# Residual stream kept feature-major in a two-block transformer kernel; the bias table loaded later

## The chip, the cores and the metric

The kernel runs on one core of one Trainium2 chip. The metric is the device time of one execution in microseconds. The time of a kernel is the median of its runs.

## The reference

Two blocks in fp32 on 256 tokens of 1024 features, cut to their lines:

```python
def first_block(x, c, ...):                       # 2 layers
    c_act = silu(c)
    for i in range(2):
        sh1, sc1, g1, sh2, sc2, g2 = split(c_act @ w_mod[i] + b_mod[i], 6)
        h = rmsnorm(x, norm_mix[i]) * (1 + sc1) + sh1
        y = pool_mixer(h, w_pool, pool_scale) if i == 0 else attention(h, w_qkv, w_o, rel_bias)
        x = x + g1 * y
        h = rmsnorm(x, norm_mlp[i]) * (1 + sc2) + sh2
        x = x + g2 * (relu(h @ w_up[i]) ** 2 @ w_down[i])      # inner width 4096
    return rmsnorm(x, norm_final)

def second_block(x, meta_tokens, ...):            # 16 meta tokens in front: 272 rows
    h = concatenate([meta_tokens, x])
    proj = rmsnorm(h, attn_norm_w) @ w_in         # gated delta rule and forgetting attention
    h = h + concatenate([o_gdn, o_fox]) @ w_out
    h = h + (silu(n @ w_gate) * (n @ w_up)) @ w_down           # n = rmsnorm(h, ffn_norm_w), 2816
    return rmsnorm(h, final_norm_w)[16:]
```

pool_mixer is a causal mean over 2, 4, 8 or 16 tokens per group of 256 features, minus the token, times a 256 x 256 matrix. The attention has 16 heads of 64 with a T5 bias that depends on the distance. rmsnorm(x, g) is x / sqrt(mean(x^2) + eps) * g over the features of a token.

## The kernel before

Some 193 MB of fp32 weights stream from HBM through four raw slots of 2 MB, in the order in which they are needed. SyncE issues the loads, each when its slot's last reader is done (`free_split`). A tile of weights is a step t (`T_POOL`, `T_MLP0 + i`, `T_QKV + i`, `T_WO`, `T_MLP1 + i`, `T_WIN + i`, `T_WOUT`, `T_FFN + i`) and goes through `split` in four quarters, two to a half: ScalarE (ACT) writes the high part `wh` (type fp32r, L568), VectorE (DVE) the rest `wl` (L1072). TensorE waits for a quarter or a half and makes three passes, high by high, low by high and high by low; `split_used` counts the halves it has read, and the next tile's split of that half waits for it. The activations are split in the same way, into `H` and `L`, both feature-major: eight blocks (k) of 128 features by 256 tokens.

In an up step (`feature_rows`, L1686) the weights are stationary and 256 tokens move: 96 matmuls of 256 columns. In a down step (`down`, L1704) the activations `aTh`, `aTl` are stationary and 512 columns of weights move: 48 matmuls, which add up in the four PSUM banks of y, token-major, over all eight downs of an MLP. The steps run up(0), up(1), down(0), up(2), down(1) and so on to up(7), down(6), down(7); MLP1 has up(8) to down(15) and the last FFN eleven pairs of half the down size. `wo_out` multiplies the mixer's output with w_o or w_out.

The residual stream `x` is token-major, two tiles of 128 tokens by 1024. Where it is updated, the work is one chain, a turn. The gate, a value per feature, is spread over the partitions: `gate_diag` makes eight diagonal matrices on DVE, `gate_mm` multiplies them with ones (L1663), `gate_copy` copies them out of PSUM. `residual` multiplies y with it, tile 0 is added by POOL (L464) and tile 1 by DVE. `stats` on ACT squares and sums a tile and takes the root, `normalise_tile` scales it on DVE, `feature_major` transposes it on TensorE in 16 transposes (L1603), `to_hf` brings it out on ACT with scale and shift (L603), and `split_h` makes `H` and `L` on DVE (L1038, L1055). Then the next tile's first matmuls can start (`parts` waits per two k). Turn 0 stands after pooling, turn 1 before QKV, turn 2 after w_o, turn 3 before W_in (two norms, one after the other, because the first block's final rmsnorm is followed by the second block's first), turn 4 after w_out, turn 5 at the end.

The order of the work is written out by hand, engine by engine. Around turn 1 ACT runs `stats(2)`, then quarters 0 and 1 of the first QKV split, `to_hf`, and quarters 2 and 3; DVE runs `residual` and `normalise_tile`, then quarters 0 and 1, `split_h`, 2 and 3. During MLP0 the modulation of layer 1 is computed too: DVE sums tiles of w_mod that lie in raw slots (`mod_halves`, L962 and L975), and TensorE adds up the partial sums in small matmuls (L1792). The start loads ten tiles of w_mod for layer 0 (`load_mod0`, matmuls L1576), the 2 MB bias table `TB` by POOL's queue from scratch (printed as `arena<-bias_rows`), x, and the pooling weights. `TB` is first read in attention. For the meta tokens the normalised rows `tokm` (DVE, semaphore `xnm_done`) are transposed in eight small transposes and put in front of the 256 tokens in `H` and `L` for W_in; before, both stand in turn 3, and ACT's statistics of them ahead of it.

## Time and profile before

| what | value |
|---|---|
| median of three runs | 1150.83 us |
| the runs | 1149.82 to 1153.22 us |
| span of the profiled execution | 1151.1 us |
| TensorE (PE) busy | 1029.5 us, 89% |
| VectorE (DVE) | 647.9 us, 56% |
| ScalarE (ACT) | 461.3 us, 40% |
| GpSimd (POOL) | 114.3 us, 10% |
| read from HBM | 193.76 MB |

The profile comes from one execution, whose own time is its span. Its first part gives the busy time of each engine; matmuls overlap, so a busy TensorE is not TensorE at its peak. The chain of waits goes from the start to the instruction that ended last and names at each step who held it up; `x96` is a count of instructions, and `out<-in` are the tiles written and read. The rows of stretches give start and end in us, the stretch, the busy us of PE, PEld, DVE, ACT and POOL with their counts, PEclk, the DMA engines' busy share and GB/s. "[2.52 <-ACT wh L568]" at the end of a row is the idle time before it and who ended it. PEclk is the granted clock of TensorE as a share of 2.4 GHz, so 0.50 is 1.2 GHz.

### The profile page before, as it was taken

The page shows a single profiled execution, that of the slowest core. Times are in us where ns is not written, and L with a number is a line of the kernel's source. Part 1 is how long each engine was busy: PE and PEld are TensorE (multiplying, and loading weights), DVE is VectorE, ACT ScalarE, POOL GpSimd, SP SyncE. Part 2 cuts the span into 40 slices and gives each one's busy share as a digit, 9 for nine tenths or more (in the row PEclk, how much of TensorE's full clock was granted, in tenths as well). Part 3 has the DMA queues.
Part 4 walks back from the last instruction along what each step waited for, and adds up shares of the span by engine and source line. Part 5 has one row for each costly group of instructions (what it writes and reads, how often), then busy time and mean ns, then how long its engine had stood idle before and what let it go on. Part 6 is the DMA issues. An engine that isn't in the chain of part 4 may idle for free.

```text
span 1151.1 us, 16537 instructions
## 1 busy us (share of the span) xinstructions
PE 1029.5 (89%) x6589; PEld 905.9 (79%) x6589; DVE 647.9 (56%) x1003; ACT 461.3 (40%) x747; POOL 114.3 (10%) x109
## 2 busy tenths in 40 slices
PE   4588999999898888899999879999579689999996
PEld 1258888997896687799889779987568669999995
DVE  1357677777555975554554556623754535554554
ACT  2234434442534222544444364553311434443443
POOL 3011110021000000111111200001443000000000
PEclk9688999999899558899999979987679899999999
DMA  9997667685637661445455524540000123555520
GB/s 339 333 384 269 220 219 272 240 278 218 236 122 241 222 220 73 147 152 213 163 202 206 181 73 147 194 133 1 1 1 1 37 73 110 175 190 182 194 98 37
DMA packets 105186, 195.60 MB, mean 170 GB/s; under 512 B 2283, under 2 KB 46572, under 8 KB 105132
## 3 DMA queue, kind: packets, MB, share of 16 engines
q1 hardware_dynamic: 104380, 192.58, 47.7%
q0 software_dynamic: 752, 2.26, 0.6%
q8 instruction: 38, 0.62, 0.2%
q14 instruction: 16, 0.13, 0.0%
HBM read 193.76 MB, written 1.07 MB: 169 GB/s over the span
## 4 chain that ended last, share of the span: by engine, by line
PE 78%; DVE 12%; DMA 3%; ACT 3%; issue 2%; POOL 1%; SPq 1%; DVEq 0%; POOLq 0%; ACTq 0%
PE ps L1686 27%; PE ps L1704 15%; PE ps L1940 7%; PE ps L2148 5%; PE ps L1632 4%; PE ps L1827 4%; DMA raw<-in_w_mod 3%; DVE wl L1072 3%; DVE accu L975 2%; ACT arena L585 1%; PE ps L2079 1%; PE ps L1576 1%; PE ps L2090 1%; POOL x L453 1%; PE ps L2089 1%
## 5 line engine op out<-in xcount | busy, mean ns | idle before, releaser
L1072 DVE TENSOR_TENSOR wl<-raw,wh 128x1024 fp32r<-128x1024 f32 (+1 forms) x288 | 315.5, 1138 | 268.4 <-ACT wh L568 268.4
L568 ACT ACTIVATE wh<-raw 128x1024 fp32r<-128x1024 f32 (+1 forms) x288 | 268.4, 983 | 355.3 <-PE ps L1686 187.2
L1686 PE MATMUL ps<-H,wh 128*128 128x256 f32 x864 | 245.0, 284 | 5.9 <-DVE L L1055 5.0
L1686 PE MATMUL ps<-H,wl 128*128 128x256 f32 x864 | 245.2, 284 | 0.0
L1686 PE MATMUL ps<-L,wh 128*128 128x256 f32 x864 | 244.9, 283 | 0.0
L1686 PEld LDWEIGHTS ps<-H,wh 128*128 128x128 f32 x864 | 165.7, 192 | 9.4 <-issue 8.4
L1686 PEld LDWEIGHTS ps<-L,wh 128*128 128x128 f32 x864 | 165.9, 192 | 0.0
L1686 PEld LDWEIGHTS ps<-H,wl 128*128 128x128 f32 x864 | 165.1, 191 | 0.9
L1704 PE MATMUL ps<-wh,aTh 128*128 128x512 f32 x256 | 102.5, 400 | 1.6 <-DVE wl L1072 1.6
L1704 PE MATMUL ps<-wh,aTl 128*128 128x512 f32 x256 | 101.8, 398 | 0.0
L1704 PE MATMUL ps<-wl,aTh 128*128 128x512 f32 x256 | 101.7, 397 | 0.0
L464 POOL TENSOR_TENSOR arena<-arena 128x512 f32<-128x512 f32 x32 | 53.8, 1681 | 310.8 <-ACT arena L613 310.8
L1940 PE MATMUL ps<-H,wh 128*128 128x272 f32 x192 | 57.6, 300 | 2.0 <-DVE L L1055 1.7
L1704 PEld LDWEIGHTS ps<-wh,aTh 128*128 128x128 f32 x256 | 48.4, 189 | 12.7 <-issue 1.6
L1704 PEld LDWEIGHTS ps<-wh,aTl 128*128 128x128 f32 x256 | 48.3, 189 | 11.9
L1940 PE MATMUL ps<-H,wl 128*128 128x272 f32 x192 | 57.3, 299 | 0.0
L1704 PEld LDWEIGHTS ps<-wl,aTh 128*128 128x128 f32 x256 | 48.5, 189 | 11.1
L1940 PE MATMUL ps<-L,wh 128*128 128x272 f32 x192 | 57.2, 298 | 0.0
L1603 PE MATMUL ps<-ident,arena 128*128 128x128 f32 x128 | 22.8, 343 | 24.3 <-DVE arena L1038 19.3
L1576 PE MATMUL ps<-raw,arena 128*32 128x512 f32 x160 | 28.6, 857 | 17.6 <-DMA raw<-in_w_mod 17.6
L1603 PEld LDWEIGHTS ps<-ident,arena 128*128 128x128 f32 x128 | 19.1, 178 | 27.9 <-DVE arena L1038 19.7
L1940 PEld LDWEIGHTS ps<-H,wh 128*128 128x128 f32 x192 | 38.0, 198 | 2.5 <-issue 2.5
(378 smaller groups left out, 1737.4 us busy)
## 6 DMA issues: line engine op xcount, KB each, us to landing
raw<-in_w_up SPq DMA_DIRECT2D x16, 2048.0 KB, 8.6
raw<-in_w_down SPq DMA_DIRECT2D x16, 2048.0 KB, 7.6
raw<-in_w_mod SPq DMA_DIRECT2D x12, 2048.0 KB, 14.9
raw<-in_w_in SPq DMA_DIRECT2D x7, 2048.0 KB, 7.8
raw<-in_w_mod SPq DMA_DIRECT2D x12, 1024.0 KB, 7.0
raw<-in_w_qkv SPq DMA_DIRECT2D x6, 2048.0 KB, 11.2
raw<-in_w_mod SPq DMA_DIRECT2D x8, 1536.0 KB, 7.0
raw<-in_w_gate SPq DMA_DIRECT2D x11, 1024.0 KB, 5.4
```

Source lines behind the costliest of these rows:

```text
L464: e.tensor_tensor(act[:, 2 * b:2 * b + 2, :], r, r, ALU.mult).then_inc(S["a_done"], 1)
L568: e.activation(dst, src, ACT.Copy).then_inc(S["split_h"], 1)
L975: ins = e.scalar_tensor_tensor(out=accu[:, u, :], in0=w[:, k, :], scalar=ccol[:, 0, k:k + 1], in1=accu[:, u, :], op0=ALU.mult, op1=ALU.add)
L1072: e.tensor_tensor(o, src, i1.bitcast(F32), ALU.subtract).then_inc(S["split_l"], 1)
L1576: ins = e.matmul(ps[g:g + 32, b, :], cpad[:, k, :], w[:, k, :], start=(k < 4), stop=(k >= 4))
L1603: ins = e.transpose(ps[:, 4 + k // 2, (k % 2) * SEQ + P * m:(k % 2) * SEQ + P * m + P], tok[:, m, P * k:P * k + P], ident[:, :])
L1632: ins = e.matmul(ps[:, bank, :], src[xa][:, 4 * hb + k, META + P * m:META + P * m + P], w[wb][:, k, :], start=(hb == 0 and k == 0 and n == 0),
L1686: ins = e.matmul(ps[:, 4 + b, SEQ * c:SEQ * c + SEQ], w[wb][:, k, P * c:P * c + P], (H, L)[xa][:, k, META:TT], start=(k == 0 and n == 0), ...
L1704: ins = e.matmul(ps[:, 2 * m + c, :], (aTh, aTl)[xa][buf][:, 2 * hb + k, P * m:P * m + P], w[wb][:, k, 512 * c:512 * c + 512], start=False ...
L1827: ins = e.matmul(ps[:, b + hb, SEQ * c:SEQ * c + SEQ], w[wb][:, k, P * c:P * c + P], (H, L)[xa][:, k, META:TT], start=(k == 0 and n == 0), ...
L1940: ins = e.matmul(ps[:, b + 2 * hb + c, 0:TT], w[wb][:, k, P * c:P * c + P], (H, L)[xa][:, k, :], start=(k == 0 and n == 0), stop=(k == KD ...
L2148: ins = e.matmul(ps[:, 2 * m + c, :], (aTh, aTl)[xa][buf][:, hb, P * m:P * m + P], (wh, wl)[wb][:, hb, 512 * c:512 * c + 512], start=False ...
```

## The change

Everything that touches the residual stream becomes feature-major: `xT`, eight blocks of 128 features by 256 tokens.

- Down steps, the FFN's downs, w_o and w_out make the weights stationary and let 256 tokens move, so that y lies feature-major in PSUM, bank b with the features of k = 2b and 2b + 1. 48 matmuls of 512 columns become 96 of 256; w_o and w_out are split in the column order (`cols=True`).
- A gate is then a scalar per partition: `residual(i, b, gate)` is one DVE instruction per k (y times gate plus x) or, without a gate, one per bank. `gate_diag`, `gate_mm`, `gate_copy` and the additions on POOL go.
- Sums of squares: `squares_of` squares a bank on ACT, `sums` adds it up on TensorE, four fp32 matmuls of two columns per bank with `onw` (ones, and the squared weight of norm_final), `root` on ACT, `rstd` on DVE, and `spread` brings the reciprocal root of each token to all partitions, two matmuls.
- `norm_out` on DVE multiplies x, the weight and the spread root per k, `high` on ACT adds the shift and writes `H`, and DVE writes `L` for k one step behind. `first_half` does the next tile's first half k by k.
- A last down is done by banks of y, with `sums` between them; the two norms of turn 3 need one pass over x, since the second sum of squares is taken with the squared weight (`second_norm`, weight product `w12`). `first_output`, which gives x its first final norm, moves from turn 3 into W_in's step 4 and is eight instructions.
- ACT's and DVE's work at turns 1 to 4 stands in a `turn` on each. In turn 1, `mods_layer1(7, 1)` moves from inside down(7) to behind it, and DVE's `mod_cols1(7)` behind the turn. In turn 0 and the turns the modulation and weight quarters are placed around `norm_out` (turn 0: DVE quarters 0 and 1 of up(0), `norm_out`, quarters 2 and 3).
- Meta tokens: DVE's `tokm` moves behind the whole split of down(14), and the transposes between up(15) and down(14); loading the meta tokens and masks moves ahead of MLP1.
- The start transposes x itself too (16 more transposes, four ACT evictions into `xT`). The table `TB` is issued on POOL behind the first `squares` instead of at the start. At the end x is transposed back in 16 transposes, and the output is stored in four parts instead of two.

```diff
...
     e.dma_start(scratch, ftab[:, :]).then_inc(S["f_out"], 16)
-    e.wait_ge(S["f_out"], 16)
-    e.dma_start(TB, bass.AP(tensor=scratch.tensor, offset=0, ap=[[1, P], [NDIST, HEADS], [1, SEQ]])
-                ).then_inc(S["tb_in"], 16)
...
             e.tensor_tensor(act[:, 2 * b:2 * b + 2, :], r, r, ALU.mult).then_inc(S["a_done"], 1)
     squares(0, first=True)
-    with e.Fori(1, 8) as j:
+    e.wait_ge(S["f_out"], 16)
+    e.dma_start(TB, bass.AP(tensor=scratch.tensor, offset=0, ap=[[1, P], [NDIST, HEADS], [1, SEQ]])
+                ).then_inc(S["tb_in"], 16)
+    with e.Fori(1, 16) as j:
         squares(j)
...
+    def squares_of(i, b):
+        e.wait_ge(S["res"], 8 * i + 2 * b + 2)
+        e.activation((sqT, sqF)[i == 5][:, 2 * b:2 * b + 2, :], xT[:, 2 * b:2 * b + 2, :], ACT.Square
+                     ).then_inc(S["sq_done"], 1)
+    def root(i):
+        e.wait_ge(S["ss_mm"], i + 1)
+        src = ps[:, ss_bank(i), 0:4].rearrange("p (m w) -> p w m", w=2)[:, 0, :]
+        e.activation(stat[:, 1, 0:NM], src, ACT.Sqrt, scale=1.0 / D, bias=epsc[:, :]).then_inc(S["rt_done"], 1)
+    def high(i, ks, shift=None):
+        for k in ks:
+            e.wait_ge(S["t_done"], 8 * i + k + 1)
+            if shift is None:
+                ins = e.activation(H[:, k, META:TT], hf[:, k, META:TT], ACT.Copy)
+            else:
+                ins = e.activation(H[:, k, META:TT], hf[:, k, META:TT], ACT.Identity, bias=shift(k))
+            ins.then_inc(S["hs_h"], 1)
...
+    def turn(i, t, slot, land, shift=None):
+        split(t, slot, land, cols=True, qs=(0, 1))
+        for b in range(4):
+            squares_of(i, b)
+        root(i)
+        high(i, range(4), shift)
+        split(t, slot, land, cols=True, qs=(2,))
+        high(i, range(4, KD), shift)
...
+    def residual(i, b, gate=None):
+        e.wait_ge(*y_ready(i, b))
+        if gate is None:
+            xb = xT[:, 2 * b:2 * b + 2, :]
+            e.tensor_tensor(xb, xb, ps[:, y_bank(i) + b, :].rearrange("p (k t) -> p k t", k=2), ALU.add
+                            ).then_inc(S["res"], 2)
+            return
+        for k in (2 * b, 2 * b + 1):
+            e.scalar_tensor_tensor(out=xT[:, k, :], in0=ps[:, y_bank(i) + b, (k % 2) * SEQ:(k % 2 + 1) * SEQ],
+                                   scalar=gate[:, k:k + 1], in1=xT[:, k, :], op0=ALU.mult, op1=ALU.add
+                                   ).then_inc(S["res"], 1)
+    def rstd(i):
+        e.wait_ge(S["rt_done"], i + 1 if i < 4 else i + 2)
+        e.reciprocal(stat[:, 2, 0:NM], stat[:, 1, 0:NM]).then_inc(S["r2_c" if i == 3 else "rs_done"], 1)
+    def norm_out(i, scale, shift=None, between=None):
+        def low(k):
+            e.wait_ge(S["hs_h"], 8 * i + k + 1)
+            if shift is None:
+                ins = e.tensor_tensor(L[:, k, META:TT], hf[:, k, META:TT], H[:, k, META:TT].bitcast(F32), ALU.subtract)
+            else:
+                ins = e.scalar_tensor_tensor(out=L[:, k, META:TT], in0=hf[:, k, META:TT], scalar=shift(k),
+                                             in1=H[:, k, META:TT].bitcast(F32), op0=ALU.add, op1=ALU.subtract)
+            ins.then_inc(S["hs_l"], 1)
+        for k in range(KD):
+            if k == 0:
+                e.wait_ge(S["bc_mm"], i + 1 if i < 4 else i + 2)
+            e.scalar_tensor_tensor(out=hf[:, k, META:TT], in0=xT[:, k, :], scalar=scale[:, k:k + 1],
+                                   in1=ps[:, ss_bank(i), SEQ:2 * SEQ], op0=ALU.mult, op1=ALU.mult
...
-        nr[0] += 1
-        e.wait_ge(S["gate_set"], gs)
-        def gated(m, c):
...
+    def turn(i, t, slot, scale, gate=None, shift=None, second=None):
+        residual(i, 0, gate)
+        split(t, slot, cols=True, qs=(0,))
+        for b in range(1, 4):
+            residual(i, b, gate)
+        split(t, slot, cols=True, qs=(1,))
+        rstd(i)
+        if second is not None:
+            second()
+        norm_out(i, scale, shift)
+        split(t, slot, cols=True, qs=(2, 3))
+    turn(1, T_QKV, landed(N_QKV)[0], mods[:, 2], modc[:, 0, 40:48], lambda k: modc[:, 1, k:k + 1])
...
     split(T_MLP1 + 14, 3)
+    e.wait_ge(S["sqm_done"], 3)
+    e.tensor_scalar(tokm, xm, stat[0:META, 2, NM:NM + 1], None, ALU.mult).then_inc(S["xnm_done"], 1)
     mlp_low(15, 1)
...
+    def first_output():
+        e.wait_ge(S["r1_set"], 1)
+        for k in range(KD):
+            e.scalar_tensor_tensor(out=xT[:, k, :], in0=xT[:, k, :], scalar=pcol[:, 1, 80 + k:81 + k],
+                                   in1=r1s[:, 0:SEQ], op0=ALU.mult, op1=ALU.mult).then_inc(S["xp_done"], 1)
+    turn(3, T_WIN, landed(N_WIN)[0], w12, modc[:, 1, 40:48], second=second_norm)
...
+    def sums(i, b):
+        e.wait_ge(S["sq_done"], 4 * i + b + 1)
+        for k in (2 * b, 2 * b + 1):
+            for m in range(NM):
+                ins = e.matmul(ps[:, ss_bank(i), 2 * m:2 * m + 2], (sqT, sqF)[i == 5][:, k, P * m:P * m + P],
+                               onw[:, k, :], start=(k == 0 and m == 0), stop=(k == KD - 1 and m == 1))
+        if b == 3:
+            ins.then_inc(S["ss_mm"], 1)
...
+    def spread(i, col=2, bank=None):
+        e.wait_ge(S["rs_done"], i + 1)
+        for m in range(NM):
+            c0 = SEQ + P * m if bank is None else P * m
+            ins = e.matmul(ps[:, ss_bank(i) if bank is None else bank, c0:c0 + P],
+                           stat[:, col, m:m + 1].broadcast_to([P, P]), ident[:, :], start=True, stop=True)
+        ins.then_inc(S["bc_mm"], 1)
...
+    def first_half(i, t, dst, c0=META, early=None):
+        w = [q[:, 0, :].rearrange("p (k n) -> p k n", k=KD) for q in (wh, wl)]
+        for k in range(KD):
+            if k % 4 == 0:
+                quarter(t, k // 4)
+            e.wait_ge(S["hs_h"], 8 * i + k + 1)
+            for c in range(2):
+                for wb in range(2):
+                    e.matmul(dst(c), w[wb][:, k, P * c:P * c + P], H[:, k, c0:TT],
+                             start=(k == 0 and wb == 0 and (c == 0 or c0 == 0)), stop=False)
+            e.wait_ge(S["hs_l"], 8 * i + k + 1)
+            for c in range(2):
+                ins = e.matmul(dst(c), w[0][:, k, P * c:P * c + P], L[:, k, c0:TT], start=False,
+                               stop=(k == KD - 1 and (c == 1 or c0 == 0)))
+                if early is not None and k == KD - 1 and c == 0:
+                    ins.then_inc(early, 1)
+        return ins
...
+        def block(hb, k, f, stop):
             w = [q[:, hb, :].rearrange("p (k n) -> p k n", k=2) for q in (wh, wl)]
-            for c in range(2):
-                for n, (xa, wb) in enumerate(PASSES):
-                    ins = e.matmul(ps[:, 2 * m + c, :], (aTh, aTl)[xa][buf][:, 2 * hb + k, P * m:P * m + P],
-                                   w[wb][:, k, 512 * c:512 * c + 512], start=False, stop=(stop and n == 2))
-                if stop and 2 * m + c < 3:
-                    ins.then_inc(S["y_done"], 1)
+            for n, (xa, wb) in enumerate(PASSES):
+                ins = e.matmul(ps[:, f // 2, SEQ * (f % 2):SEQ * (f % 2) + SEQ], w[wb][:, k, P * f:P * f + P],
+                               (aTh, aTl)[xa][buf][:, 2 * hb + k, :], start=False, stop=(stop and n == 2))
...
-                    for k in range(2):
-                        if m == 0:
-                            quarter(t, 2 * hb + k)
-                        ins = block(m, hb, k, hb == 1 and k == 1)
...
+                    block(1, 0, f, False)
+                    ins = block(1, 1, f, f % 2 == 1)
+                    if f % 2 and f < KD - 1:
+                        ins.then_inc(S["y_done"], 1)
+                    if f == KD - 1:
                         ins.then_inc(S["split_used"], 1)
-                if m == 0 and between is not None:
-                    between()
-            return
-        for hb in range(2):
...
-    down(7, 1, T_MLP0 + 15, last=True, between=lambda: mods_layer1(7, 1))
-    e.wait_ge(S["gate_set"], 4)
-    e.wait_ge(S["mod_col"], 18)
-    feature_major(xn_ready())
-    e.wait_ge(S["res_mul"], 8)
-    fresh[0] = 8
+    down(7, 1, T_MLP0 + 15, last=1)
+    mods_layer1(7, 1)
...
     up(15, T_MLP1 + 13)
+    e.wait_ge(S["xnm_done"], 1)
+    for k in range(KD):
+        ins = e.transpose(ps[:, 6, META * k:META * k + META], tokm[:, P * k:P * k + P], ident[0:META, 0:META])
+    ins.then_inc(S["mtr_done"], 1)
     down(14, 0, T_MLP1 + 14)
...
```

## Rows read from the trace of the kernel before

**Rows 1.** Page, part 1: busy us (share of the span) xinstructions, all engines

```profile
PE 1029.5 (89%) x6589; PEld 905.9 (79%) x6589; DVE 647.9 (56%) x1003; ACT 461.3 (40%) x747; POOL 114.3 (10%) x109
```

**Rows 2.** Chain that ended last, in order of time: start us, us, what; MLP1

```profile
501.24 11.20 PE ps L1704 x48
...
512.43 11.33 PE ps L1686 x96
```

**Rows 3.** Stretches: busy us PE PEld DVE ACT POOL, PEclk, DMA, GB/s

```profile
28.00:34.40 6.40, 1.77 (x16) 1.53 (x15) 0.00 (x0) 0.00 (x0) 0.00 (x0) 0.91 1.05 319
...
45.90:51.30 5.40, 3.64 (x16) 0.59 (x16) 4.36 (x3) 3.61 (x8) 0.00 (x0) 0.50 1.06 388
```

**Rows 4.** Chain in order of time, start and first up step

```profile
33.66 17.62 DMA raw<-in_w_mod
...
90.80 24.69 PE ps L1686 x192
```

**Rows 5.** DMA issues of the whole run: queue, KB each, us to landing

```profile
arena<-bias_rows POOLq DMA_DIRECT2D x1, 2048.0 KB, 15.7
```

**Rows 6.** Timeline of DVE behind turn 0: start, us, line, op, tiles, count

```profile
94.28 5.48 DVE L935 SCALAR_TENSOR_TENSOR arena<-raw,ccol,arena 128x512 f32<-128x512 f32 x7
...
99.67 2.35 DVE L1072 TENSOR_TENSOR wl<-raw,wh 128x1024 fp32r<-128x1024 f32 x2
```

**Rows 7.** Timeline of ACT, turn 0

```profile
87.14 3.75 ACT L603 ACTIVATE hf<-ps,modc,mods 128x256 f32<-128x256 f32 x8
```

**Rows 8.** Chain in order of time, MLP0 and QKV

```profile
188.97 0.78 PE ps L1792 x8
...
271.34 1.78 PE ps L1663 x16
...
294.35 48.02 PE ps L1827 x384
```

**Rows 9.** Timeline of DVE, turn 1

```profile
274.75 1.67 DVE L962 SCALAR_TENSOR_TENSOR arena<-raw,ccol,arena 128x256 f32<-128x256 f32 x4
```

**Rows 10.** Timeline of SyncE, turn 1

```profile
276.44 1.01 SPq L272 DMA_DIRECT2D raw<-in_w_qkv  x2
```

**Rows 11.** DMA issues from 276.0 to 276.5: KB each, us to landing

```profile
raw<-in_w_qkv SPq DMA_DIRECT2D x1, 2048.0 KB, 8.1
```

**Rows 12.** Stretches at turn 1, columns as rows 3

```profile
296.00:298.00 2.00, 2.00 (x11) 2.00 (x11) 1.97 (x4) 1.28 (x2) 0.00 (x0) 0.50 1.04 383
```

**Rows 13.** Chain in order of time, attention to MLP1

```profile
431.47 3.67 PE ps L1603 x16
...
442.46 12.94 PE ps L1632 x48
...
476.57 24.66 PE ps L1686 x192
```

**Rows 14.** Timeline of ACT, start of attention

```profile
366.73 1.28 ACT L695 ACT_TABLE_LOAD   x1
...
368.40 0.40 ACT L695 ACTIVATE arena<-arena,stat 128x128 f32<-128x128 f32 x1 [0.38 <-DVE stat L1231]
```

**Rows 15.** Chain in order of time, last downs of MLP1 and W_in

```profile
636.43 16.11 PE ps L1704 x69
...
673.04 14.74 PE ps L1940 x96
```

**Rows 16.** Timeline of ACT, end of MLP1

```profile
636.53 2.01 ACT L568 ACTIVATE wh<-raw 128x1024 fp32r<-128x1024 f32 x2 [2.52 <-PE ps L1686]
```

**Rows 17.** Timeline of DVE, end of MLP1 and turn 3

```profile
637.62 2.36 DVE L1072 TENSOR_TENSOR wl<-raw,wh 128x1024 fp32r<-128x1024 f32 x2 [3.32 <-ACT wh L568]
...
669.50 0.74 DVE L1302 TENSOR_SCALAR arena<-arena,stat 16x1024 f32<-16x1024 f32 x1
```

**Rows 18.** Timeline of DVE, end of the kernel

```profile
1146.78 1.28 DVE L1549 SCALAR_TENSOR_TENSOR arena<-x,stat,gate 128x1024 f32<-128x1024 f32 x1
```

More of the change, by code:

```diff
@@ L80, in build @@
         L = sb("L", [P, KD, TT], F32R)
-        gate = [sb(f"gate{i}", [P, D]) for i in range(2)]
+        mask_buf = sb("mask_buf", [P, D])
+        wrow = sb("wrow", [P, D])
         ident = sb("ident", [P, P])
@@ L723, in _ @@
                          bias=epsc[0:META, :]).then_inc(S["sqm_done"], 1)
-            stats(4)
-            stats(0, [(S["xp_done"], 1), (S["xp_done"], 2)])
+            mlp_steps(15, 1, T_MLP1 + 13, T_MLP1 + 14, landed(N_MLP1 + 14), None)
+            split(T_MLP1 + 15, *landed(N_MLP1 + 15))
             split(T_WIN, *landed(N_WIN), cols=True, qs=(0, 1))
-            to_hf(pcol[:, 1, 16:24])
-            split(T_WIN, *landed(N_WIN), cols=True, qs=(2, 3))
+            for b in range(4):
+                squares_of(3, b)
+            root(3)
+            e.wait_ge(S["r2_c"], 3)
+            e.activation(stat[:, 6, 0:NM], stat[:, 5, 0:NM], ACT.Sqrt, scale=1.0 / D, bias=epsc[:, :]
+                         ).then_inc(S["rt_done"], 1)
+            high(3, range(2))
+            e.wait_ge(S["bc_mm"], 5)
+            e.activation(r1s[:, 0:SEQ], ps[:, 6, 0:SEQ], ACT.Copy).then_inc(S["r1_set"], 1)
+            high(3, range(2, 4))
+            split(T_WIN, *landed(N_WIN), cols=True, qs=(2,))
+            high(3, range(4, KD))
+            split(T_WIN, *landed(N_WIN), cols=True, qs=(3,))
             for i in range(7):
@@ L904, in _ @@
             split(T_FFN + 21, *g_slot(N_FFN + 21), words=HALF)
-            stats(0, [(S["r2_add"], 6), (S["r2_add"], 8)])
+            for b in range(4):
+                squares_of(5, b)
+            root(5)
         @block.vector
@@ L1156, in _ @@
             scale_cols(1, 0, 112, 4)
-            split(T_MLP0, landed(N_MLP0)[0], cols=True)
-            split_h()
+            split(T_MLP0, landed(N_MLP0)[0], cols=True, qs=(0, 1))
+            e.wait_ge(S["mods_set"], 2)
+            norm_out(0, mods[:, 1], lambda k: modc[:, 0, 24 + k:25 + k])
+            split(T_MLP0, landed(N_MLP0)[0], cols=True, qs=(2, 3))
             mod_sum(10)
@@ L1295, in _ @@
[L1295 to L1302 removed]
             e.wait_ge(S["mtr_done"], 1)
[L1304 removed]
+            e.tensor_tensor(hf[:, :, 0:META], ps[:, 6, 0:KD * META].rearrange("p (k t) -> p k t", k=KD),
@@ L1689, in feature_rows, with up, down @@
                     ins.then_inc(S["split_used"], 1)
-            def up(it, t):
+            def up(it, t, turned=None):
                 first = isinstance(it, int) and it == 0
-                feature_rows(t, None if first else (S["r_done"], 2 * it - 1, "each half"))
-            def down(it, buf, t, last=False, between=None):
+                feature_rows(t, None if first else (S["r_done"], 2 * it - 1, "each half"), turned)
+            def down(it, buf, t, last=None):
                 e.wait_ge(S["tl_done"], 2 * it + 2)
-                def block(m, hb, k, stop):
+                def block(hb, k, f, stop):
@@ L1717, in down @@
+                    return ins
+                for hb in range(2):
+                    if hb == 1 and last is not None:
+                        quarter(t, 3)
+                        for f in range(KD):
+                            block(1, 0, f, False)
[3 more added lines that the diff above has]
+                            if f == KD - 1:
                                 ins.then_inc(S["split_used"], 1)
-                        if m == 0 and between is not None:
-                            between()
@@ L2163, in g_down @@
                 for hb in range(2):
                     half(t, hb)
-                    for m in range(NM):
-                        ins = block(m, hb, False)
+                    for f in range(KD):
+                        for n, (xa, wb) in enumerate(PASSES):
+                            ins = e.matmul(ps[:, f // 2, SEQ * (f % 2):SEQ * (f % 2) + SEQ],
+                                           (wh, wl)[wb][:, hb, P * f:P * f + P], (aTh, aTl)[xa][buf][:, hb, :],
+                                           start=False, stop=(last is not None and hb == 1 and f % 2 == 1 and n == 2))
+                        if last is not None and hb == 1 and f % 2 and f < KD - 1:
+                            ins.then_inc(S["y_done"], 1)
```

580 lines of the change are left out of this document (242 added, 338 removed).

## The prediction, made before the changed kernel was run

> **What bounds the kernel now.** I read the page first: TensorE is busy 89% of the span, the next engine 56% [rows 1]. That is an average over stages with different limits, so the chain of waits in order of time came next. In the MLPs it is TensorE alone, without a gap: a down step of 48 matmuls with 512 moving columns takes 11.20 us, an up step of 96 with 256 columns 11.33 [rows 2]. There only the matmuls themselves count. What is left are the start and the six places where the residual is updated and normalised ("turns": 0 after pooling, 1 before QKV, 2 before MLP1, 3 before W_in, 4 before the last FFN, 5 at the end). In the first 51 us the chain is a DMA of w_mod [rows 4], with the DMA engines full [rows 3]; at each turn TensorE stands still behind DVE and ACT and then starts at the lower clock: at 296 us the granted clock is 0.50 (1.2 GHz) although TensorE is busy again [rows 12]. I then took each turn on its engines' timelines, and its working below is a schedule by the queues as the code orders them, with these unit costs: DVE on 256 columns 1.67/4 = 0.42 us [rows 9], ACT on 256 columns with scale and bias 3.75/8 = 0.47 [rows 7], ACT and DVE per quarter of a weight split 2.01/2 and 2.36/2 [rows 16, 17], four one-column fp32 matmuls (one bank of `sums`) 0.78 [rows 8]. ACT on 512 columns in one instruction I take at 0.6, an estimate between 0.47 and the 1.0 of 1024.
>
> **Down and output weights stationary.** A down becomes 96 matmuls of 256 columns, the form of the up step: 11.33 for 11.20, +0.13 each, 16 times = +2.1; the 11 short downs of the FFN are half as large, +0.7. Together **+2.8** on the path, since nothing else is late there. Bounds: 0 (the two forms alike) and twice that.
> TensorE: Matmul & The Clock Gate, in the section Measured speedup vs the span model, of the Trainium skill says that a weight load overlaps a running matmul only where the row group differs. The change doubles the loads of a down, all of them full height. By that rule the up step, which also loads once per 256 columns, could not run at 118 ns a matmul; the trace contradicts it [rows 2], and the rival that follows from it is priced below.
>
> **The bias table loaded later.** Its 2 MB need 15.7 us in the middle of the saturated stretch [rows 3, 5]; the load rate while it runs is 319 GB/s, 388 later [rows 3]. Its bytes at the later rate are 5.4 us; with the lower rate over some 13 us (13 x (388-319)/388 = 2.3) the later w_mod tiles land up to 7.7 us earlier. What is late next: 16 more transposes of x and four ACT evictions lie before w_mod tile 3's matmuls; 16 transposes at the low clock are 3.67 us [rows 13], the evictions 2.4, but the old wait for that tile was long and only about 2 us of this stick out, on DVE's pooling chain, which had some slack. I take **-6.5** up to the pooling matmuls, bounds -3 and -8. The table now follows the first `squares`; after 100 us the engines have room, and it is read only in attention: 0, at worst 2.
>
> **Turn 0.** The gate's 16 diagonal records and copies go, but TensorE still does four sections of modulation, and now 16 `sums` (4 x 0.78 = 3.1) stand between them. My schedule has the last modulation column ready 0.5 us earlier. Then DVE's `norm_out` is 16 operations of 0.42 = 6.7 us where the old `split_h` was 4.3, and behind it in the queue stand two split quarters, the 5.9 us modulation sum and the split of the next up tile, which began at 99.67 [rows 6]. TensorE reaches that tile early and waits; the old one began up(1) near 104.1, the new one near 102.7 on the same base: **-1.4**.
>
> **Turn 1, a new wait.** `gate_mm(4)`, 1.78 us, goes [rows 8]. But ACT's `turn` now begins with the split of the first QKV tile, and ACT is in order: it first waits until that tile has landed. The tile takes the slot whose last reader is the modulation sum ending at 276.4 [rows 9]; SyncE issues it at 276.44 and it takes 8.1 us [rows 10, 11]: landed 284.5. The last down now starts at 271.34 and reaches its first `sums` (hb 0 plus four columns of hb 1, 72 matmuls) at 279.8. That sum needs ACT's squares, which are queued behind the split: 284.5 + 2.0 + 0.6 = 287.1. TensorE stands 7.3 us **inside** the down. Then, at the low clock: sums 1.8, 12 matmuls 2.5, sums 0.9, 12 matmuls 1.4, two banks of sums and the residual and square of the last bank 2.5, modulation row sum 0.8, root, reciprocal and spread 1.2: `norm_out` from 298.0. It takes 16 x 0.42, plus 0.7 for its first and last and ACT's quarter between, 7.4; the second QKV half waits for two more quarters, 2.4: 307.8, and 5.7 of matmuls: 313.5. Before, these 96 matmuls ended at 294.35 + 48.02 less the 288 that follow at 0.118 = 308.4 [rows 8]. So **+5.1**. If the tile landed before ACT asks, the same schedule gives -5.7.
>
> **Turn 2.** 431.47 to 435.14 the attention output is transposed; then came two rounds of gate matmuls with DVE copies between, until 442.46 [rows 13]. They go. With one ACT and one DVE step on 512 columns, w_o starts at 435.4: -7.0. It starts behind running transposes, so at full clock, another -1.5 (its first 48 took 12.94 for 11.2 [rows 13]). Its 192 narrow matmuls are 22.7 us; after bank 2 come 2.8 of bank 3, three banks of sums 2.5, the rest of bank 3 2.8, residual 0.9, square 0.6, last sums 0.9. ScalarE reloads its table for the square root, but that load runs ahead of the wait of its instruction (loaded at 366.73, waited until 368.40) [rows 14], so only 0.4 of its 1.3 shows; root to spread 1.2; `open_y` 1.8 at the low clock: up(8) starts at 466.8 and its first 48 matmuls end at 474.6. Before: 476.57 + 24.66 less 144 x 0.118 = 484.2 [rows 13]. **-9.6**.
>
> **Turn 3, another wait.** Counted from the start of the last down (636.43 + 11.20 = 647.63), the new schedule has its banks of sums done at 15.6, the double norm (root, five small operations, second root, spread) at 18.0, the first half at 26.7 and the second at 33.7; before it was 673.04 + 14.74, so 40.2 [rows 15]. That is -6.5. But `tokm` moved: TensorE waits for it between up(15) and down(14), and on DVE it stands behind **all four** split quarters of down(14), the last two of which can only start when up(15) is done. The last quarter ended at 637.62 + 2.36 = 639.98, 3.55 after up(15)'s end [rows 15 to 17]; `tokm` adds 0.74 [rows 17], the eight small transposes 1.0 to 1.3 (half of rows 13's, an estimate): 5.3 of TensorE at rest or at small work, plus 1.4 for the lower clock after it (at 1.2 GHz the 5 us before 299 cost about half of themselves [rows 12]; part of that time falls on the transposes). -6.5 + 5.3 + 1.4 = **+0.2**.
>
> **Turns 4 and 5.** No gate there before. Fewer evictions (-0.6) against narrow matmuls and 16 sums between: **-0.2** (bounds -2, +2). At the end 3.1 of sums and 16 transposes replace two token-wise sums of squares; the last scaled output, which ended 1.28 after 1146.78 [rows 18], I find at 1148.2: **-0.1** (bounds -2, +2).
>
> Sum: +2.8 - 6.5 - 1.4 + 5.1 - 9.6 + 0.2 - 0.2 - 0.1 = -9.7. From the execution's own 1151.1 that is 1141.4; the median of the runs is 0.3 lower: **1141**. DVE's extra `first_output` in W_in (8 x 0.42 = 3.4) falls where the convolution's 5 us stood one step before; 0, at worst 2.
>
> **Rivals.**
> 1. The two new waits don't bite (the tile is early, or ACT's order is harmless; `tokm` gets through between quarters). For: each rests on a few us of schedule. Against: the landing and the order on DVE stand in the rows [rows 9, 10, 11, 17]. Turn 1 alone: 1141 - 10.8 = 1130; turn 3 alone: 1134; both: 1123. Chance 0.14.
> 2. The start gives nothing: the transposes of x, ACT's evictions and the pooling chain take the DMA's place, or the table collides with the first MLP tiles. 1141 + 6.5 = 1147.5. For: DVE's chain there is long. Against: the w_mod tiles are awaited again and again. Chance 0.15.
> 3. Slower: `norm_out` is a ping-pong, DVE's product, ACT's high part, DVE's low part for each k. I let it overlap (0.84 per k, ACT's 0.47 hidden under the next product). If the hand-overs don't overlap, a k costs 0.42 + 0.47 + 0.42 and two hand-overs, about 1.5: 5 turns x 8 x 0.66 = +26: 1167. It decides from 1.08 per k on (9.7/40 above 0.84). Chance 0.08.
> 4. Exposed weight loads: the 768 + 264 added loads at the about 0.12 us between matmuls of the up step would be +124: 1265. Chance 0.01.
> 5. That the change doesn't do what it says would be a table still loaded in the start; that is case 2.
>
> **How the numbers follow.** Forecast 0.62, its own range 1134 to 1148 from the bounds above; rivals 0.14, 0.15, 0.08, 0.01. The range for 8 in 10 takes in turn 1's rival and case 2: 1130 to 1151. A difference under 0.3% (3.5 us) can't be told from none here: faster is below 1147.4. Of the forecast 0.58 is faster, of case 1 all, of case 2 half: 0.79; the same 0.12; slower 0.09.
>
> **What would show it.** Right: one down form at 118 ns a matmul; w_mod 3 landed before 32 us, up(0) near 82; a gap of 7 us inside the last down of MLP0 that ends with ACT's split and square; no gap between transposes and w_o; 4 us before down(14) released by DVE at the line of `tokm`. Wrong: no gap inside down(7); a k of `norm_out` over 1.0; up(0) at 90 as before.

## The result, and the profile after

The changed kernel took 1170.8 us (median of four runs, 1168.1 to 1174.2) against 1150.8: 1.0169 of the time before, 95% interval 1.0148 to 1.0189. The forecast was 1141, the range 1130 to 1151. Run again beside the last experiments it took 1166.4, 1.0115 (1.0099 to 1.0132). So it is slower by 1 to 2%, and neither the forecast nor the range held. One run of e1 (1479 us) and one of e4 (3343 us) stand in no ratio. The profiled execution has a span of 1166.4, 15.3 above the 1151.1 of before; the ledger below is made of these two.

The page's part 1 of the changed kernel, columns as [rows 1]:

```profile
PE 1059.1 (91%) x7917; PEld 992.8 (85%) x7917; DVE 635.4 (54%) x1002; ACT 460.3 (39%) x733; POOL 101.9 (9%) x101
```

The other engines have less to do than before, TensorE 29.6 more. The added matmuls of the downs are not the reason: in MLP1 five pairs of steps take 113.3 for 112.7. The chain of waits, in order of time (start, duration, what), by turn:

```profile
66.90 4.52 PE ps L1628 x32
71.42 3.61 PE ps L1594 x16
...
99.38 1.42 DVE arena L966
...
116.05 11.30 PE ps L1742 x96
...
288.10 2.00 ACT wh L574 x2
...
290.67 1.87 PE ps L1628 x8
292.54 2.77 PE ps L1742 x12
...
315.58 40.03 PE ps L1859 x336
...
449.47 6.86 PE ps L1688 x48
...
507.13 11.30 PE ps L1742 x96
...
646.67 1.45 DVE arena L1300
648.17 1.03 PE ps L1928 x8
649.20 20.31 PE ps L1742 x156
...
951.21 3.35 PE ps L1628 x24
954.56 5.34 PE ps L1696 x24
```

L1628 is `sums` (a fp32 matmul has two records, so x8 is one bank), L1742 the down step, L1594 the modulation rows, L1859 QKV, L1300 `tokm`, L1696 w_out. Where such landmarks stand in both chains, the span can be cut into stretches:

| stretch | before | after | difference | forecast |
|---|---|---|---|---|
| start to turn 0's gate (DVE's product of gate and scale) | 64.5 | 60.9 | -3.7 | -6.5 |
| to down(0): turn 0, up(0), up(1) | 51.0 | 55.2 | +4.2 | -1.4 |
| down(0) to down(5) | 121.1 | 122.9 | +1.8 | +0.6 |
| down(5) to QKV's fifth tile: turn 1 | 105.8 | 116.7 | +10.9 | +5.5 |
| to the attention output's transposes: code not changed | 89.1 | 90.0 | +0.9 | 0 |
| to down(8): turn 2 | 69.8 | 61.6 | -8.2 | -9.6 |
| down(8) to down(13) | 112.7 | 113.3 | +0.6 | +0.6 |
| down(13) to the end of W_in: turn 3 | 152.0 | 154.7 | +2.7 | +0.6 |
| to w_out: nearly all of it code not changed | 152.3 | 154.6 | +2.3 | 0 |
| w_out to the FFN's first down: turn 4 | 58.9 | 62.1 | +3.2 | -0.2 |
| the rest | 174.1 | 174.6 | +0.5 | +0.6 |

The misses have one thing in common, which the rows of stretches show (start:end, stretch, busy us of PE, PEld, DVE, ACT and POOL with counts, PEclk, DMA share, GB/s). Of the changed kernel:

```profile
66.80:71.40 4.60, 4.60 (x37) 4.58 (x41) 0.00 (x0) 1.07 (x3) 0.00 (x0) 0.77 1.05 386
71.40:83.60 12.20, 10.77 (x50) 4.65 (x49) 0.17 (x1) 3.25 (x5) 0.00 (x0) 0.50 0.87 311
...
290.60:302.00 11.40, 11.20 (x52) 11.11 (x52) 3.48 (x7) 1.91 (x4) 0.00 (x0) 0.50 1.05 387
302.00:311.00 9.00, 7.80 (x36) 7.53 (x36) 4.75 (x13) 3.93 (x8) 0.00 (x0) 0.50 0.09 33
...
951.20:954.60 3.40, 3.40 (x26) 3.32 (x26) 0.79 (x2) 1.23 (x2) 0.00 (x0) 0.82 0.76 239
954.60:959.90 5.30, 5.29 (x24) 4.99 (x24) 0.00 (x0) 0.00 (x0) 0.00 (x0) 0.50 0.00 0
```

In the first row TensorE is busy all the time, with `sums`, and the granted clock falls from 1.0 to 0.50 (1.2 GHz) inside it. In the third and fourth it stays at 0.50 for 20 us though TensorE works. In the last two it falls during w_out's sums, and there TensorE is busy without a gap from 937 on; in turn 0 it had stood still for 0.7 us until 65.9. Summed over stretches of 2 us, (1 - PEclk) x 2 x PE busy gives the microseconds that TensorE worked at the low clock: 176 before, 206 after. At half speed 29.4 more are 14.7 us of time. That this is close to the 15.3 of the spans is in part chance: the second profile of the changed kernel (e10) has 200, 11.9 us of time, where its span is 18.1 longer. The ledger's misses hold waits as well.

Theory: the two-column matmuls of `sums` leave or keep TensorE at the low clock. Rival: the idle time around each turn does, and the sums' shape is of no matter. Beside it stand the two waits of the forecast, in turns 1 and 3, and the table's place.

### The profile page after: what moved, and what is told of

The parts are those of the page before. It is cut to its first block, busy times and chain, and to the rows that moved or that the text cites. A ratio compares the mean times of both kernels' runs of the same rounds, so it can differ in the third digit from the quotient of the medians.

```text
span 1166.4 us, 19172 instructions
## 1 busy us (share of the span) xinstructions
PE 1059.1 (91%) x7917; PEld 992.8 (85%) x7917; DVE 635.4 (54%) x1002; ACT 460.3 (39%) x733; POOL 101.9 (9%) x101
## 4 chain that ended last, share of the span: by engine, by line
PE 78%; DVE 13%; ACT 3%; DMA 3%; issue 2%; SPq 1%; POOL 0%; DVEq 0%; ACTq 0%
PE ps L1725 23%; PE ps L1742 14%; PE ps L1969 6%; PE ps L2175 5%; PE ps L1859 3%; PE ps L1696 3%; DVE wl L1114 3%; DMA raw<-in_w_mod 2%; PE ps L1628 2%; PE ps L1668 2%; DVE accu L1006 2%; PE ps L1651 1%; PE ps L1594 1%; PE ps L1688 1%; PE ps L2108 1%
## 5 line engine op out<-in xcount | busy, mean ns | idle before, releaser
L1114 DVE TENSOR_TENSOR wl<-raw,wh 128x1024 fp32r<-128x1024 f32 (+1 forms) x288 | 316.8, 1141 | 278.7 <-ACT wh L574 278.7
L1725 PE MATMUL ps<-H,wh 128*128 128x256 f32 x816 | 228.6, 280 | 2.5 <-DVE wl L1114 1.6
L1725 PE MATMUL ps<-H,wl 128*128 128x256 f32 x816 | 229.7, 282 | 0.0
L1725 PEld LDWEIGHTS ps<-H,wh 128*128 128x128 f32 x816 | 154.2, 189 | 3.2 <-issue 3.2
L1742 PE MATMUL ps<-aTh,wh 128*128 128x256 f32 x512 | 147.4, 288 | 1.6 <-DVE wl L1114 1.6
L1742 PE MATMUL ps<-aTh,wl 128*128 128x256 f32 x512 | 146.2, 285 | 0.0
L1742 PE MATMUL ps<-aTl,wh 128*128 128x256 f32 x512 | 145.9, 285 | 0.0
L1742 PEld LDWEIGHTS ps<-aTh,wh 128*128 128x128 f32 x512 | 99.5, 194 | 1.6 <-issue 1.6
L1742 PEld LDWEIGHTS ps<-aTl,wh 128*128 128x128 f32 x512 | 99.3, 194 | 0.0
L1742 PEld LDWEIGHTS ps<-aTh,wl 128*128 128x128 f32 x512 | 99.3, 194 | 0.0
L2175 PE MATMUL ps<-aTh,wh 128*128 128x256 f32 x176 | 49.3, 280 | 0.0
L2175 PE MATMUL ps<-aTh,wl 128*128 128x256 f32 x176 | 49.1, 279 | 0.0
L2175 PE MATMUL ps<-aTl,wh 128*128 128x256 f32 x176 | 49.1, 279 | 0.0
L1628 PE MATMUL ps<-onw,arena 128*128 128x2 f32 x192 | 28.2, 274 | 12.8 <-ACT arena L594 12.7
```

Of the source, the lines that this page charges most:

```text
L1114: e.tensor_tensor(o, src, i1.bitcast(F32), ALU.subtract).then_inc(S["split_l"], 1)
L1628: ins = e.matmul(ps[:, ss_bank(i), 2 * m:2 * m + 2], (sqT, sqF)[i == 5][:, k, P * m:P * m + P], onw[:, k, :], start=(k == 0 and m == 0), s ...
L1725: ins = e.matmul(ps[:, 4 + b, SEQ * c:SEQ * c + SEQ], w[wb][:, k, P * c:P * c + P], (H, L)[xa][:, k, META:TT], start=(k == 0 and n == 0), ...
L1742: ins = e.matmul(ps[:, f // 2, SEQ * (f % 2):SEQ * (f % 2) + SEQ], w[wb][:, k, P * f:P * f + P], (aTh, aTl)[xa][buf][:, 2 * hb + k, :], st ...
L2175: ins = e.matmul(ps[:, f // 2, SEQ * (f % 2):SEQ * (f % 2) + SEQ], (wh, wl)[wb][:, hb, P * f:P * f + P], (aTh, aTl)[xa][buf][:, hb, :], st ...
```

## The experiments

**The sums by themselves (e7, e8).** 32 fp32 matmuls that compute nothing, between down(13) and up(15), where TensorE never idles; two moving columns, then 64:

```diff
+            for n in range(32):
+                e.matmul(ps[:, 7, 0:2], ident[:, :], onw[:, 0, :], start=True, stop=True)
             up(15, T_MLP1 + 13)
```

> Changed kernel with 32 extra fp32 matmuls of 2 moving columns, reading constants and written to an unused bank, between down(13) and up(15), in a stretch where TensorE is never idle and the granted clock is 1.0. It measures the sums by themselves. Theory A: the granted clock falls to 0.50 during or right behind them though TensorE is never idle: the matmuls cost 6.2 at full clock, and they and the first microseconds of up(15) take 3 to 6 more: 1180 to 1184. Theory B (only idle time lowers the clock): clock stays 1.0, 6.2 more, 1177.

> As e7, but each of the 32 matmuls moves 64 columns. Theory A: the clock stays at 1.0, and as each matmul is bounded by its issue or load at about 0.2 us, the cost is the 6.2 to 6.9 of the matmuls alone: 1177.5. Theory B: the same as e7. If e7 and e8 both lose the clock, 64 columns are too few as well, and e1's gain has another cause.

Measured: 1185.2 and 1177.3 us (two runs each), 1.0291 and 1.0222 of before. Chain and stretches of e7, then of e8:

```profile
635.99 11.22 PE ps L1926 x64
647.21 13.66 PE ps L1725 x96
...
631.00:636.00 5.00, 5.00 (x46) 5.00 (x44) 2.36 (x2) 1.39 (x2) 0.00 (x0) 1.00 0.88 338
636.00:641.00 5.00, 5.00 (x35) 5.00 (x35) 2.46 (x3) 3.34 (x5) 0.00 (x0) 0.73 0.11 15
641.00:647.20 6.20, 6.20 (x31) 6.20 (x30) 0.00 (x0) 0.00 (x0) 0.00 (x0) 0.50 0.88 329
```

```profile
630.95 7.09 PE ps L1926 x64
638.04 11.43 PE ps L1725 x96
...
631.00:634.50 3.50, 3.50 (x34) 3.50 (x33) 2.43 (x3) 3.32 (x5) 0.00 (x0) 1.00 0.02 5
634.50:638.00 3.50, 3.50 (x33) 3.50 (x33) 0.04 (x1) 0.00 (x0) 0.00 (x0) 1.00 0.69 211
```

With two columns the clock falls to 0.50 while TensorE is 100% busy, and 32 times more moving columns cost less: 7.09 for 11.22, and the up step behind them 11.43 for 13.66. That is theory A, by 6.4 us in the profiles. The Trainium skill (TensorE: Matmul & The Clock Gate, section Why this matters for your kernels) names idle gaps between matmul bursts as what to avoid; here there is none, and the measurement decides: narrow matmuls alone are enough.

**Wide sums in the kernel (e1).**

```diff
-                        ins = e.matmul(ps[:, ss_bank(i), 2 * m:2 * m + 2], (sqT, sqF)[i == 5][:, k, P * m:P * m + P],
-                                       onw[:, k, :], ...
+                        ins = e.matmul(ps[:, ss_bank(i), 64 * m:64 * m + 64], (sqT, sqF)[i == 5][:, k, P * m:P * m + P],
+                                       onw[:, k, :].unsqueeze(2).broadcast_to([P, 2, 32]), ...
```

> Changed kernel (median 1170.8) with one edit: each matmul of `sums` moves 64 columns (each of the two weights 32 times) instead of 2; the number of matmuls stays, and only one copy of each result is read. Theory A: the 16 two-column matmuls of each turn count as almost no work for the clock gate, so the granted clock falls to 0.50 while TensorE is busy (turn 0 from 68 us on, turn 4 at 954) or stays there (turn 1 from 290 to 310). In the changed kernel 19 us of busy time in turn 0, 20 in turn 1 and 18 in turn 4 run at the low clock, before it was 6, 7 and 15; at 64 columns most of it goes and half of each microsecond comes back: about 6 + 5 + 2, so 1158. Theory B: the clock is low because TensorE stood idle before each turn, and how wide the sums are does not matter: 1171, the granted clock as in the changed kernel. If the wider matmuls cost more than the narrow ones, the 24 quarters of sums show it: each of the 96 matmuls of turns 0 to 5 took 0.195 us at full clock.

Measured: 1158.3 us, 1.0045 (1.0023 to 1.0067), 12 below the changed kernel's first median and 8 below its second. By stretches: gate to down(0) 52.8 for 55.2, turn 1 113.9 for 116.7, turn 4 59.3 for 62.1. Its w_out keeps the full clock, sums and matmuls behind them:

```profile
946.40:949.30 2.90, 2.90 (x26) 2.82 (x26) 0.78 (x2) 1.23 (x2) 0.00 (x0) 1.00 0.98 308
949.30:952.20 2.90, 2.86 (x24) 2.66 (x23) 0.00 (x0) 0.00 (x0) 0.00 (x0) 1.00 0.00 1
```

The rival falls for turn 4: its stretch took 62.1 or 62.2 in all eight profiles with narrow sums and 59.3 or 59.4 in all four with wide ones. In turn 0 the wide sums did not hold the clock in this profile:

```profile
69.20 4.87 PE ps L1628 x32
```

They held it in e5 (3.62) and e6 (3.63) and not in e12 (6.04), while it fell inside the narrow ones in all eight profiles. One-column modulation sums stand before and behind them, so that the width alone decides there is not shown. Nor is it in turn 1, where the narrow profiles lie between 114.4 and 116.7.

**Turn 1's wait (e2).**

```diff
 def turn(...):      # ACT, for i == 1
-    split(t, slot, land, cols=True, qs=(0, 1))
     for b in range(4):
         squares_of(i, b)
     root(i)
+    split(t, slot, land, cols=True, qs=(0, 1))
```

and on DVE, for i == 1:

```diff
     residual(i, 0, gate)
-    split(t, slot, cols=True, qs=(0,))
     for b in range(1, 4):
         residual(i, b, gate)
-    split(t, slot, cols=True, qs=(1,))
     rstd(i)
+    split(t, slot, cols=True, qs=(0, 1))
```

> Changed kernel with one edit: in turn 1 ACT does its four squares and the root before quarters 0 and 1 of the first QKV split, and DVE takes its two quarters behind the reciprocal. Theory A: in the changed kernel TensorE stands from 282.4 to 290.7 inside the last down because ACT waits for the QKV tile, which lands at 288.1, and then works at the low clock until 310. Without the wait the sums end near 287, both quarters are split by 291.3 and the second QKV half starts near 301 instead of 315.6: 1157. Rival: the tile lands at 288.1 whatever is done, its splits, norm_out and the clock decide; then the gain is 3 us or less, 1168 or more.

Measured: 1151.1 us, 1.0017 (0.9984 to 1.0049), 20 below the changed kernel's first median and 15 below its second. Chain:

```profile
263.03 18.49 PE ps L1749 x156
281.55 0.89 DVE xT L1074 x2
283.14 1.05 PE ps L1635 x8
284.20 1.52 PE ps L1749 x12
...
303.94 40.03 PE ps L1866 x336
```

The 8.3 us at rest inside the last down are gone, 12 matmuls take 1.52 where they took 2.77, and down(5) to QKV's fifth tile is 104.5 for 116.7 (114.4 to 116.7 in the seven profiles with narrow sums and without the edit). The rival (the tile's landing decides) falls. Another 5.9 of this profile's 16.5 are in the stretch W_in to w_out, 148.7 for 154.6, which the edit doesn't touch.

**`tokm` early (e3).** On DVE:

```diff
             e.reciprocal(stat[0:META, 2, NM:NM + 1], stat[0:META, 1, NM:NM + 1]).then_inc(S["sqm_done"], 1)
-            split(T_MLP1 + 14, 3)
             e.wait_ge(S["sqm_done"], 3)
             e.tensor_scalar(tokm, xm, stat[0:META, 2, NM:NM + 1], None, ALU.mult).then_inc(S["xnm_done"], 1)
+            split(T_MLP1 + 14, 3)
```

> Changed kernel with one edit: DVE's reciprocal and `tokm` (the meta tokens) stand before the four split quarters of down(14) instead of behind them. Theory A: TensorE's 6.1 us between up(15) (ends 643.1) and down(14) (starts 649.2) are DVE's last two quarters and `tokm`; with `tokm` early only the 1.0 of small transposes stays, and the 1.4 to 1.9 lost to the lower clock behind the gap go too: 6 to 7 us less, 1164.5. Rival: down(14) would have waited for its own split anyway, or the time is given back at the last down's banks: under 2 us, 1169 or more.

Measured: 1159.9 us, 1.0074 (1.0046 to 1.0102), 11 below the changed kernel's first median and 6 below its second, whose interval it touches. The stretch of turn 3 is what shows the gain: 145.9, where the six profiles without the edit or added matmuls lie between 154.6 and 154.8. Chain, up(15) and then the downs:

```profile
632.66 11.36 PE ps L1725 x96
644.62 18.58 PE ps L1742 x156
```

0.6 instead of 6.1 lies between them, the transposes in it, and 156 matmuls take 18.58 for 20.31, as the clock no longer falls.

**The table's place (e4, e9).** Undone in the changed kernel, and made alone in the kernel before:

```diff
             squares(0, first=True)
+            e.wait_ge(S["f_out"], 16)
+            e.dma_start(TB, ...).then_inc(S["tb_in"], 16)
```

> Changed kernel with one part undone: the bias table is loaded at the start again, as in the kernel before. Theory A: the later table brings the pooling forward by 3.7 us (its last DVE step at 61.0 instead of 64.7), but in turn 0 the loss at the low clock eats it, and up(1) starts where DVE's queue lets it; undoing it costs the 3.7 again: 1174.5. Rival: DVE's modulation sum and splits behind turn 0 set up(1) in any case, and the table's place is worth nothing: 1171.

> Kernel before (1150.8) with only the bias table's load moved behind the first `squares` of POOL, nothing else of the change. e4 put the table's place at 5.6 to 6.9 us within the changed kernel. Theory: that is the start's DMA alone, and it holds on the kernel before as well: down(0) starts 5 to 6 us earlier, 1145. Rival: on the old turn 0 the next modulation tiles or DVE's sum and splits stand in its way and less than 2 us reach down(0): 1149 or more. The stretch from the end of W_in to w_out is the same code in all these kernels and took 152.3 before, 148.7 to 156.0 in eight profiles of changed ones; here it gives a second sample on the old code.

Measured: e4 1177.4 us, 1.0194 (1.0159 to 1.0229), its gate at 67.8 for 60.9 and 63.3 in the two profiles of the changed kernel; e9 1142.6 us, 0.9897 (0.9864 to 0.9930), faster than the kernel before. Chain of e9:

```profile
29.07 16.36 DMA raw<-in_w_mod
45.47 3.69 PE ps L1576 x16
...
81.58 25.13 PE ps L1686 x192
106.71 11.20 PE ps L1704 x48
```

The w_mod tile awaited until 51.3 [rows 4] is there at 45.4, 5.9 earlier; the gate stands at 57.95 for 64.53, down(0) at 106.7 for 115.5. So the table's place is worth 6.6 to the gate, and all of the rest of the change costs 24 to 28 us: 1166.4 to 1170.8 against 1142.6.

**The changed kernel again (e10).**

> The changed kernel as it is, once more, beside e9 on the same chip. It says how far segments of unchanged code move from one profile to the next: expected 1171, down(0) at 116 to 118, W_in to w_out 149 to 156 with 46 to 60 us of busy time at the low clock. If that stretch is at 154 to 156 again and e9's is at 152, its 2 us belong to the change; if they overlap they belong to the clock's phase.

Measured: 1166.4 us, profile 1169.2. Gate at 63.25 for 60.85: in this execution the first 16 transposes ran at the low clock. W_in to w_out took 156.1 here and 156.1 in e9, which has the old code; over the twelve profiles of the changed kernel and its edits it lies between 148.7 and 156.1. Old code 152.3 and 156.1, new code on both sides of that: those 2.3 us can't be put down to the change. The attention's stretch took 90.0 in e9 as well. Turn 2's stretch was 63.6 here and 61.6 in the first profile, and in the old code 67.9 (e9) and 69.8; down(1) took 12.8 here, 14.2 in the first profile.

**The start's transposes (e11).** On TensorE, and the same call removed from its old place:

```diff
             mod_mm(0)
+            feature_major([(S["x_in"], 16)] * 2, [(S["f_sb"], 1), (S["pcopied"], 2)], src=x_tok)
             mod_rows(2)
```

> Changed kernel with one edit: the start's 16 transposes of x itself stand behind the second modulation tile, where TensorE waits some 5.6 us for the third (20.1 to 25.6), instead of behind that third tile. Theory: in the profiles of the changed kernel these 16 transposes and ACT's evictions of them lie on the path: from the third tile's landing to the first `mods` it takes 13.5 to 15.8 us, in the kernel before with the later table 10.1 (25.73 to 35.83). Taken off the path, the gate of turn 0 (`mods` at 60.85 to 63.3) comes at 57 to 58 and down(0) at 112.5 to 113.5: 3.4 to 5 less than the changed kernel, 1164 (its medians were 1170.8 and 1166.4). Rival: the pooling chain has slack, or the 3 us are lost again at turn 0's modulation tiles: under 1 us.

Measured: 1167.3 us, 1.0138 (1.0102 to 1.0174), no gain that can be told from the changed kernel's two medians. Gate at 60.4, not 57 to 58: TensorE now ran at the low clock between 24 and 32 us, and turn 0's sums again:

```profile
24.00:28.00 4.00, 2.24 (x12) 0.59 (x16) 0.46 (x1) 1.42 (x3) 0.00 (x0) 0.54 1.05 341
28.00:32.00 4.00, 4.00 (x21) 2.67 (x14) 0.00 (x0) 0.60 (x1) 0.00 (x0) 0.50 1.06 371
...
67.84 5.96 PE ps L1629 x32
```

**Together (e5, e6, e12).** e5 has the edits of e1, e2 and e3. e6 adds this on DVE behind turn 0; e12 adds e11's edit to e6.

```diff
+            split(T_MLP0 + 1, landed(14)[0], cols=True, qs=(0, 1))
             mod_sum(10)
-            split(T_MLP0 + 1, landed(14)[0], cols=True)
+            split(T_MLP0 + 1, landed(14)[0], cols=True, qs=(2, 3))
```

> Changed kernel with the edits of e1 (64-column sums), e2 (squares first in turn 1) and e3 (`tokm` early) together. By segments of the profiles: turn 1 116.7 to about 104, turn 2 -1.0, turn 3 154.7 to 145.9, turn 4 62.1 to 59.3, the first two downs -1 to -2. Theory A (three separate losses, which add): 12.5 + 1 + 8.8 + 2.8 + 2 = 27 below the changed kernel, 1143.5, below the kernel before (1150.8). Rival: e1's gain in turn 1 and e2's are the same microseconds (the low clock behind the wait), and e2's median held some 6 us of unchanged code at a better clock: then 1147 to 1150, no better than before.

> e5 with one more edit: behind turn 0 DVE splits quarters 0 and 1 of up(1) before the modulation sum instead of after it. Theory: in the changed kernel TensorE was done with up(0) at 101.7 and began up(1) at 104.4, because DVE's queue held norm_out (6.9), two quarters (2.4) and the sum (6.6) ahead of that split; with the quarters first up(1) starts when up(0) ends, 2.7 less than e5. Rival: the sum's slot is freed 2.4 later, the load behind it too, and down(0) or down(1) waits for its tile or split: 0 or slower.

> e6 (64-column sums, squares first, `tokm` early, turn 0's split order) with e11's edit. Theory: the start's 3.4 us come on top, as TensorE then only meets turn 0 earlier: e6's 1137.3 becomes 1133.5, and against the kernel before the ratio is 0.985. Rival: in e6 the first w_up tile is already awaited at 77.5 by ACT's split of up(0), so DMA decides from there and at most 1 us is left: 1136 to 1137.

Measured: 1139.9 us, 0.9896 (0.9873 to 0.9918); 1137.3, 0.9888 (0.9845 to 0.9931); 1142.8, 0.9899 (0.9866 to 0.9932). e5 lies 30.9 below the changed kernel's first median, 26.5 below its second and 11 below the kernel before. Taken alone the three edits gave 29.7 against that second median and 42.9 against the first, so the medians say only roughly that the losses add. The profile of e5 says it by stretches: gate to down(0) 49.4 for 55.2, turn 1 104.6 for 116.7, turn 2 60.4 for 61.6, turn 3 147.5 for 154.7, turn 4 59.4 for 62.1, with the gate itself 2.4 later: 26.5, the difference of the two spans. The losses are separate. e6 is not told apart from e5: the split no longer waits, and a tile does. e12 has its gate 2.9 before e6's and then turn 0 at the low clock, so that the w_up tile is issued at 109.5 for 103.6: in this profile it loses more than it gained. Turn 0's sums in e5, then the chain of e6, then that of e12:

```profile
69.50:73.10 3.60, 3.60 (x37) 3.53 (x39) 0.00 (x0) 0.97 (x2) 0.00 (x0) 1.00 1.05 385
```

```profile
103.59 12.64 DMA raw<-in_w_up
```

```profile
65.15 6.04 PE ps L1637 x32
71.19 3.62 PE ps L1602 x16
...
109.49 12.58 DMA raw<-in_w_up
```

## Why the prediction was wrong, step by step

- **Down and output weights stationary, +2.8:** right. 0.12 per pair of steps in MLP1, 0.08 per pair in the FFN; no weight load shows between the matmuls. (The rule on row groups that the prediction quotes from the Trainium skill stands in TensorE: Matmul & The Clock Gate under The mechanism, not under the section named.)
- **The table, -6.5 to the pooling matmuls:** the table's own part was right (e9: 6.6 to the gate). Wrong was what should stick out of the added transposes of x, "about 2 us": the gate of the changed kernels stands 2.9 to 5.3 behind e9's. The transposes run between the third tile's landing and the modulation sums, and at either clock. The table's 7.7 less these 2 was 5.7 in any case; the step to 6.5 rested on a slack that the gates don't show.
- **Turn 0, -1.4:** the failed step, a term priced at the wrong clock. "16 `sums` (4 x 0.78 = 3.1)" priced the sums at full clock and let everything behind them run at it. They took 4.5, the clock fell inside them, and the two modulation tiles behind took 3.6 each at the low clock where they took 1.9. The DVE queue that I named (`norm_out`, two quarters, sum, split) then set up(1) at 104.4, where 96.2 was forecast with the start's term (102.7 less 6.5). Where the clock held through turn 0, in e5, gate to down(0) took 49.4; the forecast comes to 49.6 (51.0 less 1.4), against 55.2 measured in the changed kernel. So most of what was missing in this term is the clock, as far as one profile says it.
- **Turn 1, +5.1:** the mechanism was right in each link: the tile issued at 279.4, landed at 288.1, TensorE at rest from 282.4 to 290.7 inside the last down. 10.9 was measured, 5.4 more: the wait was 8.3 for 7.3, and from the first sums to `norm_out` it took 15.2 for 10.9, because I let the clock come back before `norm_out`; between single banks of matmuls and narrow sums it stayed at 0.50 until 311. In e10 it came back near 301 and fell again by 306, and the stretch took 114.8. Without the wait e2 gains 12.2 against the first profile, where rival 1 had priced it at 10.8; but against the kernel before it is only 1.3 shorter, where 5.3 was forecast for the stretch without the wait (5.7 less 0.4 for the downs).
- **Turn 2, -9.6:** the way was right, the size less sure than -8.2 looks: the second profiles of both codes, e10 and e9, give -4.3. The clock decides: in the kernel before it was 0.50 at w_o's start and 1.0 in e9, and in e10 it fell inside the sums. The steps of the recorded schedule add up to 466.4, not 466.8, for up(8).
- **Turn 3, +0.2:** the wait for `tokm` was right and 0.8 longer than forecast (6.1 for 5.3), the low clock behind it too. Taken out, turn 3 is 6.1 below the kernel before, where -6.5 was forecast for the turn without the wait.
- **Turn 4, -0.2:** measured +3.2, of which e1 gives back 2.8: the sums ahead of the last 24 matmuls, the same failed step as in turn 0, and here with the width shown to decide.
- **`norm_out`, rival 3:** not the cause. A k takes 0.79 in the changed kernel (0.84 forecast), with ACT's step hidden:

```profile
88.28 0.47 DVE L1093 SCALAR_TENSOR_TENSOR hf<-xT,mods,ps 128x256 f32<-128x256 f32 x1
88.67 0.48 DVE L1087 SCALAR_TENSOR_TENSOR L<-hf,modc,H 128x256 fp32r<-128x256 f32 x1
89.07 0.47 DVE L1093 SCALAR_TENSOR_TENSOR hf<-xT,mods,ps 128x256 f32<-128x256 f32 x1
```

  The result fell near this rival's 1167 by another mechanism, one that stood among none of the rivals: added work on TensorE that lowers its clock.

The misses add up: 5.6 in turn 0's stretch, 2.8 in the start, 5.4 in turn 1, 3.4 in turn 4, 2.1 in turn 3, 1.4 in turn 2, 1.2 in the first downs and 3.2 in code that didn't change, less 0.1 in the rest: 25.0, which is 15.3 measured less the -9.7 forecast. That the low clock in the first downs (a down at 14.2 for 13.0) comes from the change is not shown; at 12.8 in e10 it need not. Turn 0 with its one-column modulation sums made wide as well was not tried.

## What to carry to other kernels

A small matmul is not priced by its own duration: count what its shape does to TensorE's clock, and how many microseconds of full-size work stand behind it at half speed. When sums over partitions are moved to TensorE, try giving them columns, even useless ones: 64 for 2 cost less time in e8 and in every turn 4 here, though between one-column matmuls they held the clock only in two profiles of four. When an engine's program is reordered, put what other engines wait for ahead of a split that itself waits, for a DMA in turn 1 and for the up step before it in turn 3; two such moves, each of a few lines, were worth 12 and 9 us, and a transfer moved out of a saturated start 10.
